# The boundary between stages, with GpSimd as a third adder, and four edits of order

## The reference, cut to what matters

```python
m = c_act @ w + b                              # adaLN: shift, scale, gate from the condition c
h = x * rsqrt(mean(x * x, axis=-1) + eps) * g  # RMSNorm over the 1024 channels
h = h * (1.0 + scale) + shift
x = x + gate * block(h)                        # the ffn blocks of the first part: 0.5 * gate
```

## Time and profile before

| what | value |
|---|---|
| median of the runs | 1783.66 us (1782.2 to 1787.7) |
| the profiled execution's own time | 1789.82 us |
| its span | 1788.0 us |
| PE busy | 1747.4 us (98%) |
| DVE busy | 1453.3 us (81%) |
| ACT busy | 958.2 us (54%) |
| POOL busy | 0.2 us (4 instructions) |
| mean granted TensorE clock | 0.996 of full speed |

### The profile page before, as it was taken

The page is one execution under the profiler, slowest core; times in us unless marked ns, Lnnn a source line. Parts: engine busy times, 40 slices in busy tenths (PEclk is TensorE's granted clock), DMA queues, the critical chain, the costliest instruction groups (busy, mean ns, idle before and its releaser), DMA issues.

```text
span 1788.0 us, 34255 instructions
## 1 busy us (share of the span) xinstructions
PE 1747.4 (98%) x14686; PEld 1698.2 (95%) x14686; DVE 1453.3 (81%) x1749; ACT 958.2 (54%) x1254; POOL 0.2 (0%) x4
## 2 busy tenths in 40 slices
PE   4999999999999999999999999999999999999999
PEld 4999999998999999999999999999999998989999
DVE  7799898888899989897658999765899887567766
ACT  4444566665544454445765333565655556775553
POOL 0000000000000000000000000000000000000000
PEclk9999999999999999999999999999999999999999
DMA  9998744443698959894435979343388535426551
GB/s 394 414 419 330 301 142 165 151 157 141 243 419 330 360 201 387 326 389 177 154 136 220 391 308 356 138 148 139 114 303 289 211 143 179 151 73 214 188 196 37
DMA packets 68150, 426.23 MB, mean 238 GB/s; under 512 B 7489, under 2 KB 10833, under 8 KB 31825
## 3 DMA queue, kind: packets, MB, share of 16 engines
q1 hardware_dynamic: 63936, 416.22, 61.1%
q10 hardware_dynamic: 4112, 8.62, 1.4%
HBM read 423.74 MB, written 3.17 MB: 239 GB/s over the span
## 4 chain that ended last, share of the span: by engine, by line
PE 92%; ACT 3%; DVE 3%; DMA 2%; issue 1%; DVEq 0%; ACTq 0%; SPq 0%
PE bank L1563 24%; PE bank L1564 24%; PE bank L1565 24%; PE bank L1616 2%; PE bank L1618 2%; PE bank L1617 2%; PE bank L1576 1%; PE bank L1672 1%; PE bank L1590 1%; PE bank L1972 1%; DMA mix<-mods 1%; PE bank L1579 1%; ACT w_hi L495 1%; DMA biases<-scratch 1%; PE bank L1806 1%
## 5 line engine op out<-in xcount | busy, mean ns | idle before, releaser
L1563 PE MATMUL bank<-h_hi,w_hi 128*128 128x256 f32 x2504 | 695.4, 278 | 0.9 <-DVE h_lo_rest L1172 0.9
L1564 PE MATMUL bank<-h_lo_rest,w_hi 128*128 128x256 f32 x2504 | 693.7, 277 | 0.0
L1565 PE MATMUL bank<-h_hi,w_lo 128*128 128x256 f32 x2504 | 693.7, 277 | 0.0
L913 DVE TENSOR_TENSOR w_lo<-raw,w_hi 128x2048 fp32r<-128x2048 f32 x267 | 610.2, 2287 | 94.4 <-ACT w_hi L495 93.3
L495 ACT ACTIVATE w_hi<-raw 128x2048 fp32r<-128x2048 f32 x276 | 528.4, 1914 | 157.3 <-PE bank L1565 137.6
L1563 PEld LDWEIGHTS bank<-h_hi,w_hi 128*128 128x128 f32 x2504 | 471.9, 188 | 1.1 <-DVE h_lo_rest L1172 1.1
L1564 PEld LDWEIGHTS bank<-h_lo_rest,w_hi 128*128 128x128 f32 x2504 | 470.2, 188 | 0.0
L1565 PEld LDWEIGHTS bank<-h_hi,w_lo 128*128 128x128 f32 x2504 | 470.1, 188 | 0.0
L1563 PE MATMUL bank<-a_hi,w_hi 128*128 128x256 f32 x1280 | 357.3, 279 | 0.2 <-DVE a_lo L1284 0.2
L1564 PE MATMUL bank<-a_lo,w_hi 128*128 128x256 f32 x1280 | 354.6, 277 | 0.0
L1565 PE MATMUL bank<-a_hi,w_lo 128*128 128x256 f32 x1280 | 354.6, 277 | 0.0
(11 more groups left out here) (299 smaller groups left out, 1998.5 us busy)
## 6 DMA issues: line engine op xcount, KB each, us to landing
raw<-weights SPq DMA_DIRECT2D x276, 1024.0 KB, 5.2
modws<-mods SPq DMA_DIRECT2D x144, 768.0 KB, 6.8
mix<-mods SPq DMA_DIRECT2D x5, 1024.0 KB, 8.8
mix<-mods ACTq DMA_DIRECT2D x8, 512.0 KB, 13.5
biases<-scratch ACTq DMA_DIRECT2D x1, 2048.0 KB, 14.0
mix<-biases ACTq DMA_DIRECT2D x4, 512.0 KB, 4.0
modws<-mods SPq DMA_DIRECT2D x1, 1024.0 KB, 12.2
x<-xin SPq DMA_DIRECT2D x1, 1024.0 KB, 10.9
```

The costliest lines, as they stand in the source:

```text
L913: eng.tensor_tensor(w_lo[g % NW][:, :], raw[g % NRAW][:, :], w_hi[g % NW][:, :], ALU.subtract).then_inc(sems["wlo"], 1)
L1563: eng.matmul(dst, ah, bh, start=start, stop=False, skip_group_check=skip)
L1564: eng.matmul(dst, ah, bl, start=False, stop=False, skip_group_check=skip)
L1565: return eng.matmul(dst, al, bh, start=False, stop=stop, skip_group_check=skip)
```

## The change

Boundary, for stages 0, 2, 3, 4, 6, 7 and 8: in the last out block tile 6 comes first and has its own `pair`; tile 7 comes alone at the end. The adds of squares leave DVE; GpSimd has a program of its own with five adds, and PE's products of squares go from five to three. Order: the adaLN sums of stages 3, 4, 6 and 8 come one out block earlier on PE, and before the last `split` and `lo` on DVE; in the last group of stage 7 `lo` stands before `split`; sb's group 1 has `arg` between its two splits; dsa's group 0 has scores of heads 0 and 1 before the query squares of heads 2 and 3; V's gemm has the product with `h`'s low part first at kk = 0.

```diff
+def out_order(st):
+    if st + 1 >= len(STAGES) or STAGES[st] == "mamba" or st + 1 == RESCALED:
+        return tuple(range(KT))
+    return 6, 0, 1, 2, 3, 4, 5, 7
+def six_first(st):
+    return out_order(st)[0] == 6
 ...
@@ scalar: norm
-                for m in range(KT):
+                for n, m in enumerate(out_order(st - 1) if st else range(KT)):
                     if st:
-                        k.wait("xup", st - 1, b=m)
+                        k.wait("xup", st - 1, b=n)
@@ vector: residual
-                for two in ((0, 1), (2, 3), (4, 5), (6, 7)):
-                    if summed and two[0] == (6 if final else 4):
+                turns = ((6,), (0, 1), (2, 3), (4, 5), (7,)) if six_first(st) else ((0, 1), (2, 3), (4, 5), (6, 7))
+                for n, two in enumerate(turns):
+                    if final and two[0] == 6:
                         add_squares(0, 1)
-                    if summed and two[0] == 6 and not final:
-                        add_squares(2, 3)
-                        add_squares(0, 2)
-                    if two[0] < 6:
-                        k.wait("pair", st, b=two[0] // 2)
+                    if two[-1] < 7:
+                        k.wait("pair", st, b=n)
 ...
@@ vector: ffn, and likewise cffn
                 def down(i, a, b):
+                    if i == NFB - 1 and 0 < st < NST - 1:
+                        modulation(st + 1)      # in cffn then: lo(i), split(st, i, a, b)
                     split(st, i, a, b)
                     lo(i)
@@ vector: attention body
                     split(st, i, a, b)
+                    if kind == "sb" and i == 1:
+                        arg(i, 0)
+                        arg(i, 1)
                     split(st, i, a, b + 1)
 ...
-                    if more:
+                    if kind == "sb" and i > 1:
                         arg(i, 0)
                         arg(i, 1)
@@ gpsimd: new
+            def add(st, m, other):
+                k.inc("sqa", eng.tensor_tensor(work3[:, m, :], work3[:, m, :], work3[:, other, :], ALU.add))
+            for st in range(1, NST):
+                if six_first(st - 1):
+                    k.wait("sq", st, b=1)
+                    add(st, 0, 6)
+                    k.wait("sq", st, b=3)
+                    add(st, 1, 2)
+                    k.wait("sqa", st, b=1)
+                    add(st, 0, 1)
+                    k.wait("sqa", st, b=2)
+                    k.wait("sq", st, b=4)
+                    add(st, 0, 3)
+                    k.wait("sq", st, b=6)
+                    add(st, 4, 5)
@@ tensor: gemm
+                            if tokens and kk == 0:
+                                eng.matmul(d, h_lo(kk)[:, part], hi[:, kk, :], start=True, stop=False)
+                                eng.matmul(d, h_hi[:, kk, part], hi[:, kk, :], start=False, stop=False)
+                                eng.matmul(d, h_hi[:, kk, part], lo[:, kk, :], start=False, stop=False)
+                            elif tokens:
@@ tensor: summed_squares
-                order = [(0, 0), (2, 1), 4, 5, 6, 7] if kinds == 2 else [4, 5, (0, 2), 6, 7]
+                order = [(0, 0), (2, 1), 4, 5, 6, 7] if kinds == 2 else [(0, 3), (4, 4), 7]
@@ tensor: ffn, ahead of the last down
+                if 0 < st < NST - 1:
+                    modulation(st + 1)
@@ tensor: last
-                for m in range(KT):
+                for m in out_order(st):
                     if m == 6 and more and token:
                         squares(st + 1, 0)
+                    if m == 7 and six_first(st):
+                        k.wait("xup", st, b=0)
 ...
-                    if m in (1, 3, 5):
+                    if m in (1, 3, 5) or m == 6 and six_first(st):
                         k.inc("pair", mm)
@@ tensor: dsa, group 0
-                        query_squares(i)
+                            query_squares(i, (0, 1))
+                            scores(i, (0, 1))
+                            query_squares(i, (2, 3))
+                            scores(i, (2, 3))
```

More of the change, by code:

```diff
@@ L186, in steps @@
         g = GROUPS[kind]
-        out = {"fold": 4 if st else 0, "mods": 1, "modv": 1, "pair": 3, "xup": 8, "sq": 8, "ss": 1, "ln": 1, "rstd": 1,
+        out = {"fold": 4 if st else 0, "mods": 1, "modv": 1, "pair": 4 if six_first(st) else 3, "xup": 8, "sq": 8, "ss": 1, "ln": 1, "rstd": 1,
                "t": 8, "hhi": 8, "hlo": 8, "ahi": 0, "alo": 0}
         if st and self.stages[st - 1] != "mamba":
-            out |= {"sqa": 4 if st == RESCALED else 3}
+            out |= {"sqa": 4 if st == RESCALED else 5}
         if st == RESCALED:
@@ L1066, in residual @@
                 nxt = st + 1
-                summed = nxt < NST and not token
                 final = nxt == RESCALED
                 def add_squares(m, other):
[L1071 to L1075, removed]
+                    for r in range(2):
+                        k.wait("sq", nxt, b=2 * other + r)
                         s = sq2 if r else work3
                         k.inc("sqa", eng.tensor_tensor(s[:, m, :], s[:, m, :], s[:, other, :], ALU.add))
-                for two in ((0, 1), (2, 3), (4, 5), (6, 7)):
-                    if summed and two[0] == (6 if final else 4):
+                turns = ((6,), (0, 1), (2, 3), (4, 5), (7,)) if six_first(st) else ((0, 1), (2, 3), (4, 5), (6, 7))
+                for n, two in enumerate(turns):
+                    if final and two[0] == 6:
                         add_squares(0, 1)
-                    if summed and two[0] == 6 and not final:
-                        add_squares(2, 3)
-                        add_squares(0, 2)
-                    if two[0] < 6:
-                        k.wait("pair", st, b=two[0] // 2)
+                    if two[-1] < 7:
+                        k.wait("pair", st, b=n)
                     else:
@@ L1097, in residual @@
                             scalar=modv[:, st, 16 + m:17 + m], in1=x[:, m, :], op0=ALU.mult, op1=ALU.add))
-                if summed and final:
+                if final:
                     add_squares(2, 3)
@@ L1175, in down @@
                 def down(i, a, b):
-                    split(st, i, a, b)
-                    lo(i)
+                    if i == NFB - 1 and 0 < st < NST - 1:
+                        modulation(st + 1)
+                        lo(i)
+                        split(st, i, a, b)
+                    else:
+                        split(st, i, a, b)
+                        lo(i)
                 gate(0, 0, 0)
@@ L1538, in _ @@
                 programs[kind](st)
-                if st + 1 < NST and kind != "dsa":
+                if st == 0 or kind in ("mamba", "moba", "sb"):
                     modulation(st + 1)
                 residual(st)
+        @block.gpsimd
+        def _(eng):
+            k = Steps(eng, plan, sems)
+            def add(st, m, other):
[13 more added lines that the diff above has]
+                    add(st, 4, 5)
         @block.tensor
@@ L1611, in gemm @@
                                 eng.wait_ge(sems["wlo"], k.block(st, b=1) + 1)
-                            if tokens:
+                            if tokens and kk == 0:
[3 more added lines that the diff above has]
+                            elif tokens:
                                 mm = three(d, h_hi[:, kk, part], h_lo(kk)[:, part], hi[:, kk, :], lo[:, kk, :],
@@ L1742, in last @@
                                stop=True).then_inc(sems["gmods"], 1)
-                if more and not early:
+                if more and not early and (st == 0 or not ffn):
                     modulation(st + 1)
@@ L1883, in heads, with query_squares @@
                 n = GROUPS[kind]
-                def query_squares(i):
+                def query_squares(i, heads=(0, 1, 2, 3)):
                     k.wait("ptc", st, i, 4, -2)
-                    for h in range(4):
+                    for h in heads:
                         if h % 2 == 0:
@@ L1893, in query_squares, with scores @@
                                             start=True, stop=True)
-                    k.inc("qss", mm)
-                def scores(i):
+                    if heads[-1] == 3:
+                        k.inc("qss", mm)
+                def scores(i, heads=(0, 1, 2, 3)):
                     free = {4: ("alo", 2, -1), 5: ("vev", 1, 0), 6: ("ptc", 4, -1), 7: ("ptc", 4, -2)}
@@ L1903, in scores @@
                         free[4], free[5] = ("ol", 2, -1), ("alo", 2, -1)
-                    k.wait("qev" if kind != "dsa" else "qev2", st, i, 1, 0)
+                    k.wait("qev" if kind != "dsa" or heads == (0, 1) else "qev2", st, i, 1, 0)
                     if kind != "dsa":
                         k.wait("kev", st, i, 1, 0)
-                    for h in range(4):
+                    for h in heads:
                         to = score_bank(kind, i)[h]
@@ L2007, in body @@
                             values(i, 1)
-                        query_squares(i)
-                        if more:
```

(9 more changed lines are left out.)

## The result

The changed kernel takes 1805.5 us in the median of four runs (1803.8 to 1806.2), the kernel before 1785.7 (four runs, 1782.2 to 1788.6): a ratio of 1.0107 [1.0081, 1.0133]. The forecast was 1785.6 us with a range up to 1798.5. The profiled execution shown here took 1804.86 us, with a span of 1803.1.

The account below looks back on a forecast made before the run. PE's list of products was taken to bound the kernel (busy 1747.4 of 1788.0 us). The terms +4.7 - 0.9 - 1.2 - 0 - 0.7 = +1.9 us gave 1785.6 us on the median, range 1778 to 1798.5.

Parts of the forecast that it names:

- +4.7: Seven changed boundaries together: Ln at T0+3.27 instead of 2.60, 0.67 later each, so 4.7 us lost.
- Ln = T0+0.67+4g: Boundary: start of ACT's Ln when the chain of five GpSimd adds sets it; T0+3.27 expected, against 2.60 before.
- T0: Zero of time at a boundary: start of the products of squares, when tile 7's last matmul has been issued.
- g: Time of one GpSimd add of squares at the boundaries, taken as 0.65 us; break-even 0.48.
- the lock: Boundaries: DVE's late_split and a GpSimd add exclude each other for a whole instruction; the case of the first rival.
- the first rival: Boundaries: late_split shuts out the fifth add, (4,5); Ln at T0+5.0, 16.9 us over seven, 1797.8 us total; chance 0.20.
- Were nothing else in the chain, Ln would start at T0+1.97: 4.4 us over seven.: Boundaries: tile 6 first and adds off DVE end tile 7's square earlier, winning 0.63 us each time.
- cffn -0.9: Stage 7's last group: lo ahead of split removes PE's wait for the low part; 0.9 us won.
- sb -1.2: sb's group 1: arg between the two splits comes 2.3 us earlier, PE's wait for pt goes; 1.2 us won.
- adaLN sums hidden: Ffn stages: 1.2 us of small DVE instructions ahead of the last split fit where DVE waits for ACT; no cost.
- dsa 0: dsa's group 0: scores fill PE's 1.2 us wait, but PE waits 1.1 longer later; 0 won, 1.1 at best.
- V -0.7: V's gemms, low part first: steps of 0.340 instead of 0.354 in some 12 slow half gemms; 0.7 us won.

Follow-up runs that it names:

- experiment 1: Changed kernel, but DVE's late_split at the seven boundaries waits for GpSimd's fifth and last add; 1790.0 us, ratio 1.0028.
- experiment 2: Changed kernel plus 20 unused fill products on PE ahead of the products of squares, late_split not delayed; 1798.6 us, ratio 1.0086.
- Experiment 5: Changed kernel without GpSimd: tile 6 still first, three adds of squares on DVE, five products on PE; 1781.6 us, ratio 0.9988 to the kernel before.
- experiment 9: Changed kernel with an unused one-input DVE reduction in late_split's place, late_split waiting for the fifth add; 1788.5 us, ratio 1.0017.
- experiment 6: Changed kernel with four GpSimd adds (tiles 4 and 5 not added), four products, late_split waiting for the fourth add; 1781.3 us, ratio 0.9988.

## Why the prediction was wrong

By its own steps, at the seven boundaries (+23.8 us where it had +4.7):

- *"Ln = T0+0.67+4g", g = 0.65.* The formula is sound: with the lock away, g = 0.73 gives T0+3.59, and experiment 1 had 3.4 to 3.8 (4.1 after stage 8). The adds' price was too low by 0.08, which counts four times at each boundary, 2.2 us over seven: 6.9 by the formula, +6.5 measured, instead of +4.7. This is the small part.
- *The lock, the first rival, chance 0.20.* It is what happened, and it is the step that failed: it should have been the forecast. It had 0.20 because no row showed GpSimd beside DVE, and because the fifth add might have followed the fourth at once. But the fifth was not the one hit. The first add, called early, began only at T0-1.36 and held up the rest by 0.3; so the fourth was ready at T0+0.95, and the split, at T0+0.68, stood ahead of it. Five adds and one split of 1.75 on one line of time would have shown that the split meets one of them in any order: from T0-0.7 the adds stand one behind the other until T0+2.3. Its cost was 10.2 us. The rival's own price was right, though by the wrong add: it had 16.9 us over seven boundaries for lock and adds together, and experiment 2, which keeps both and takes the clock's fall away, has 50.6 - 33.9 = 16.7. The Trainium skill (SBUF — State Buffer, section Who interferes with whom) had the rule, that a VectorE instruction with two SBUF inputs contends with a GpSimd one that reads SBUF and that the second is blocked wholly. The traces agree: 2.12 against 0.73 for the blocked add, a split of 2.19 against 1.75 where the add was first, and no delay beside the one-input reduction. In both cases the second ends 0.1 to 0.2 us sooner than a full wait and its whole length would make.
- *The clock: not in the sum, nor in any rival.* 7.1 us. A gap of 3 us was in the first rival's own working (Ln at T0+5.0 with two products left), and what a gap does to TensorE's clock wasn't asked. With it that rival gives about 1805, the time measured.
- *"Were nothing else in the chain, Ln would start at T0+1.97: 4.4 us over seven."* Wrong, and hidden by the loss. Experiment 5 takes GpSimd away and wins 0.8 over seven boundaries, since five products fill T0 to T0+2.4 whatever DVE does. What bounds the boundary is PE's own products of squares and the hand-over to ACT behind them.

Outside the boundaries most steps held as far as they can be measured. *cffn -0.9*: the wait is gone, -0.7 to -0.8. *sb -1.2*: the wait is gone, -1.5 with stage 5. *adaLN sums hidden*: no wait came in their place. *dsa 0*: so, 137.9 to 138.6 with the edit and 137.9 to 138.3 without; where its waits stand changes with the execution. *V -0.7*: this step failed. The stage came out 0.4 to 0.6 shorter in the changed kernel, but its gemms step at 0.354 throughout and not at 0.34, so the size is luck. Two of its readings were off as well: fourteen half gemms were slow, not twelve, and the low part first did not bring the fast step. With the profile of before at the stage 5 pitch of most executions the sum is 23.9 - 3.4 = 20.5, and the medians differ by 19.8; some 2 of the 3.4 are the edits', 1.4 are stage 0's.

## What to carry to other kernels

Before work is moved to GpSimd, lay its instructions beside every DVE instruction of two SBUF inputs in the same microseconds. A 0.73 us add took 2.1 when it came second, and a chain of adds that runs without a break across the start of such an instruction was blocked at all seven boundaries; one wait that keeps the DVE instruction behind the chain took that back. Where TensorE will stand for some microseconds, price the clock's fall too, here 1 us each time; here it was more than half as dear as the lock that caused the gap. And before a latency is shortened, ask what ends next in the chain: here five products of PE stood right behind the wait that was removed, and 4.4 us of expected gain came to 0.8. Last, a gain of the right size is no proof of its reason: V's edit had one and its gemms had become no faster.

## What the runs showed of the hardware

- A GpSimd add of 128x256 in f32 takes 0.73 us (729 and 731 ns mean in experiments 1, 9 and 6), DVE's 0.43; from add to add through a semaphore GpSimd lost 0.08.
- TensorE's clock fell to 0.50 after gaps of 3 us at seven of seven boundaries, and after gaps of 1.6 and 1.8 us at two of seven in experiment 9, while a gap of 2.2 in the same execution and all of experiment 1's (1.4 to 2.1) left it at 1.00. What decides at such a length stays open.
- One kernel has executions in which a whole stage of matmuls runs 3% slower at the same granted clock (0.1176 against 0.1143 us each). It belongs to the execution, not to the program: times of the kernel before gather near 1783, 1788.5 and 1794.5. Its cause stays open; a difference of 5 us between two single profiles must be checked against it, stage by stage, before a reason is sought.
